# Output's start overlapped with the end of decode, and decode's joint sums moved into the output slabs

## The chip, the cores and the metric

One core of one Trainium2 chip runs the whole kernel. The metric is the device time of one execution in microseconds, lower is better. Engines are named as the profile names them: PE (TensorE), DVE (VectorE), ACT (ScalarE), POOL (GpSimd), SP (SyncE, here the queue that issues nearly all DMAs).

## What is computed

One decoder layer on 512 prompt rows and 8 x 4 sample rows, model width 2048, float32. An input projection feeds three mixers: differential attention (A, 4 heads), sparse attention (B, 4 heads, three branches) and an mLSTM (C, 8 heads). The last stages of the kernel, which the change touches, are the decode attention of the samples and the output product:

```
oa = rms_norm(oa, a_out_g) * (1.0 - lam_init)
ya = oa * silu(az)                      # group A
yb = (sum over 3 branches of gate * o_branch) * silu(bz)   # group B, gate = sigmoid(bg)
yc = rms_norm(h, c_out_g) * gates       # group C
y  = x + concat(ya, yb, yc) @ w_out     # (544, 2048) @ (2048, 2048)
```

The decode attention runs each sample batch over 4096 cached keys in pages, and its partial softmaxes are joined with running maxima and sums at the end.

## The kernel before, in words

The program is a chain of stages; each stage (`Stage`) frees its semaphores and ends with a barrier of all engines (line 94). The order of the work inside a stage is written out by hand for each engine, which is an in-order queue; semaphores tie them together.

**Decode** (`decode_attend`, line 1594). It goes through N = 80 steps: 8 batches with eight groups of four pages, one window and one step of new rows each. Each step loads its pages (2.5 MB, SP), turns keys (PE), scores, takes maxima (DVE), exponentials (ACT), turns them back and sums the values (PE, lines 1829 to 1845); ACT copies the sums out (`copy_o`). Per batch DVE combines the partial results in seven parts (`finish`, lines 2044 to 2077): weights, two scalings of `ob` (line 2071, nine and eleven columns of 128) and three sums (line 2076). After the last batch come the joint sums over the branches: transposes of maxima and sums (lines 1876, 1877), a joint exponential (1972), the scaling of `os_` (2121), six gathers of 512 columns on PE (1879, 1887) with copies on ACT and DVE, and twelve stores of 16 KB to `o_att` by SP (1727), awaited.

**Output** (`output`, line 3074). w_out's 2048 columns are cut into four slabs of 512 (j = 0 to 3), its 2048 rows into eight chunks of 256 (c = 0 to 7); a group is g = 8 j + c. Weights are split into a high half in the short matmul format (`high_w` on ACT, line 3279) and a low half (`low_w` on DVE, 3366), the activations likewise (`mhi`, `mlo`), and each product is three matmuls (3442 to 3444), so that a group costs 4 tiles x 2 x 3 = 24 matmuls of 512 columns. The rows come in five tiles: 0 to 3 of the prompt, and tile 4 with the 32 sample rows (`TURN`, `LAST` = 4). A tile is loaded (`load_tile`: `hc` 512 KB, `att` 1 MB, `zab` 512 KB, `zc` 2 x 256 KB, two buffers), POOL applies the gates to `att` (3254), ACT squares twelve heads and takes one root (`norms`, 3264 to 3271), DVE mixes (`mix`, 3322 to 3346: reciprocal, four products, three operations on group B, eight products on C), PE turns four quarters of it (`turn`, 3432), ACT and DVE make the high and low halves (`high`, `low`, 3288 and 3359).

Slab 0 goes tile by tile, since tile t + 1 is being mixed while tile t is multiplied: it is turned after chunk 5 of tile t. Slabs 1 to 3 go chunk by chunk with all four tiles in each. The sample rows (tile 4) are turned in slab 1's first group and multiplied by the unsplit weights, 16 small matmuls (3454) a group; for slab 0, which they missed, the weights are loaded a second time into one buffer `wx` and multiplied every third group. `add_x` (3368) adds x to a finished tile's product and so frees its PSUM bank; the first product of the next slab waits for it (3474). SP stores y and reads the next x in the second group of each slab (3193 to 3196, 3187), each read waiting for its own store to have landed. SP issues a weight chunk four groups ahead, once its buffer has been used (3175).

## Time and profile before

| what | us |
|---|---|
| three runs, median (lowest to highest) | 1827.3 (1820.32 to 1835.65) |
| profiled execution, span of its instructions | 1829.8 |
| PE busy in it | 1633.6 |
| output stage, from its first load (1582.1) to the end | 247.7 |

The profiled execution's time outside its span is not recorded. In windows the columns are the stretch, its length, then busy us (x instructions) of PE, PE weight loads, DVE, ACT and POOL, the granted PE clock as a share of full speed, the share of the DMA engines' time in use and GB/s. In timelines the columns are start, duration, engine, line, operation, written <- read, shapes, count, and in brackets the idle time before it with what ended it. In the chain they are start, duration, engine, tile and line. In the page's fifth part they are the group, then busy us and mean ns of one, then idle us before it and what ended most of it. In the DMA table they are the issue, its count, its size and the median us from issue to landing.

### The profile page before, as it was taken

The page shows a single profiled execution, that of the slowest core. Times are in us where ns is not written, and L with a number is a line of the kernel's source. Part 1 is how long each engine was busy: PE and PEld are TensorE (multiplying, and loading weights), DVE is VectorE, ACT ScalarE, POOL GpSimd, SP SyncE. Part 2 cuts the span into 40 slices and gives each one's busy share as a digit, 9 for nine tenths or more (in the row PEclk, how much of TensorE's full clock was granted, in tenths as well). Part 3 has the DMA queues.
Part 4 walks back from the last instruction along what each step waited for, and adds up shares of the span by engine and source line. Part 5 has one row for each costly group of instructions (what it writes and reads, how often), then busy time and mean ns, then how long its engine had stood idle before and what let it go on. Part 6 is the DMA issues. An engine that isn't in the chain of part 4 may idle for free. (4 is left out here: it accounts for less than half of the span.)

```text
span 1829.8 us, 38972 instructions
## 1 busy us (share of the span) xinstructions
PE 1633.6 (89%) x14817; PEld 1261.7 (69%) x14817; DVE 794.7 (43%) x1568; ACT 603.9 (33%) x1383; POOL 121.0 (7%) x186
## 2 busy tenths in 40 slices
PE   6999999999998899998977789899988988289998
PEld 5888888877777767776656666667666776067776
DVE  4212121263247444433435444665566556473221
ACT  4311121232122222321224154555555554252110
POOL 3000000053000001000012000000000000120000
PEclk9999999999999999998987698999999999589999
DMA  6556565685332324255246488999998996382343
GB/s 200 177 176 198 180 193 152 219 283 183 138 109 94 117 87 148 79 129 172 65 132 250 168 293 333 336 351 391 346 327 330 386 325 233 143 290 87 129 140 118
DMA packets 219686, 375.37 MB, mean 205 GB/s; under 512 B 42197, under 2 KB 122630, under 8 KB 218190
## 3 DMA queue, kind: packets, MB, share of 16 engines
q1 hardware_dynamic: 215390, 359.78, 57.7%
q0 software_dynamic: 3824, 11.02, 1.8%
q8 instruction: 118, 1.93, 0.4%
q10 hardware_dynamic: 288, 2.10, 0.4%
q14 instruction: 66, 0.54, 0.1%
HBM read 336.37 MB, written 40.71 MB: 206 GB/s over the span
## 5 line engine op out<-in xcount | busy, mean ns | idle before, releaser
L377 PE MATMUL pj_ps<-pj_whi,pj_xhi 128*128 128x512 f32 (+1 forms) x1024 | 413.7, 404 | 6.9 <-PEq L94 6.0
L378 PE MATMUL pj_ps<-pj_wlo,pj_xhi 128*128 128x512 f32 (+1 forms) x1024 | 399.3, 390 | 0.0
L379 PE MATMUL pj_ps<-pj_whi,pj_xlo 128*128 128x512 f32 (+1 forms) x1024 | 398.0, 389 | 0.0
L295 DVE TENSOR_TENSOR pj_wlo<-pj_w,pj_whi 128x1024 fp32r<-128x1024 f32 (+1 forms) x128 | 155.6, 1215 | 453.8 <-ACT pj_whi L253 452.1
L253 ACT ACTIVATE pj_whi<-pj_w 128x1024 fp32r<-128x1024 f32 (+1 forms) x128 | 132.2, 1033 | 506.0 <-DMA pj_w<-in_w_in 505.2
L377 PEld LDWEIGHTS pj_ps<-pj_whi,pj_xhi 128*128 128x128 f32 x1024 | 195.6, 191 | 66.5 <-issue 28.9
L379 PEld LDWEIGHTS pj_ps<-pj_whi,pj_xlo 128*128 128x128 f32 x1024 | 195.9, 191 | 40.2
L378 PEld LDWEIGHTS pj_ps<-pj_wlo,pj_xhi 128*128 128x128 f32 x1024 | 195.9, 191 | 33.9
L1899 ACT ACTIVATE da_kT<-da_tp 128x512 f32<-128x512 f32 x200 | 119.5, 597 | 176.6 <-PE da_tp L1766 165.5
L1991 DVE COPY da_kT<-da_tp 128x512 f32<-128x512 f32 x128 | 88.4, 690 | 91.8 <-PE da_tp L1766 91.3
L3442 PE MATMUL ou_ps<-ou_whi,ou_mhi 128*128 128x512 f32 x256 | 104.8, 409 | 6.7 <-DVE ou_wlo L3366 6.7
L3443 PE MATMUL ou_ps<-ou_wlo,ou_mhi 128*128 128x512 f32 x256 | 101.8, 397 | 0.0
L3444 PE MATMUL ou_ps<-ou_whi,ou_mlo 128*128 128x512 f32 x256 | 100.9, 394 | 0.0
L1766 PE MATMUL da_tp<-all_ident,at_early_a 128*128 128x128 f32 x512 | 77.5, 292 | 13.9 <-DMA at_early_a<-in_cache_a_kv 11.8
L3366 DVE TENSOR_TENSOR ou_wlo<-ou_w,ou_whi 128x1024 fp32r<-128x1024 f32 x32 | 40.6, 1287 | 97.5 <-ACT ou_whi L3279 97.4
L1766 PEld LDWEIGHTS da_tp<-all_ident,at_early_a 128*128 128x128 f32 x512 | 60.5, 149 | 23.9 <-DMA at_early_a<-in_cache_a_kv 15.4
L1766 PE MATMUL da_tp<-all_ident,da_pa 128*128 128x128 f32 x512 | 72.9, 279 | 2.1 <-DVE da_kT L1991 1.8
L1780 PE MATMUL da_sa<-da_kT,at_qa 128*32 128x512 f32 x512 | 68.8, 609 | 4.2 <-ACT da_kT L1899 4.2
L3279 ACT ACTIVATE ou_whi<-ou_w 128x1024 fp32r<-128x1024 f32 x32 | 33.5, 1058 | 112.7 <-DMA ou_w<-in_w_out 108.9
L2006 DVE TENSOR_REDUCE da_nm<-da_sa 128x1 f32<-128x512 f32 x64 | 44.1, 689 | 60.8 <-PE da_sa L1780 60.6
L343 PE MATMUL pj_ps<-pj_w,pj_xs 128*32 128x128 f32 (+1 forms) x2048 | 67.7, 273 | 0.0
L1766 PEld LDWEIGHTS da_tp<-all_ident,da_pa 128*128 128x128 f32 x512 | 56.2, 141 | 12.9 <-issue 6.3
(552 smaller groups left out, 2217.1 us busy)
## 6 DMA issues: line engine op xcount, KB each, us to landing
at_early_a<-in_cache_a_kv SPq DMA_DIRECT2D x128, 512.0 KB, 6.6
da_pa<-in_cache_a_kv SPq DMA_DIRECT2D x128, 512.0 KB, 6.4
pj_w<-in_w_in SPq DMA_DIRECT2D x120, 512.0 KB, 4.6
px_pages<-in_cache_b_kv SPq DMA_DIRECT2D x256, 128.0 KB, 2.5
at_early_b<-in_cache_b_kv SPq DMA_DIRECT2D x128, 128.0 KB, 6.4
da_pb<-in_cache_b_kv SPq DMA_DIRECT2D x128, 128.0 KB, 6.5
ou_w<-in_w_out SPq DMA_DIRECT2D x32, 512.0 KB, 4.2
proj<-pj_out SPq DMA_DIRECT2D x52, 256.0 KB, 4.9
```

The source lines that it names most:

```text
L253: act.activation(self.whi[:, g % self.RING, :, 0:n], self.w[:, g % self.RING, :, 0:n], ACT.Copy).then_inc(self.whi_ready, 1)
L295: dve.tensor_tensor(self.wlo[:, r, :, 0:n], self.w[:, r, :, 0:n], self.whi[:, r, :, 0:n], ALU.subtract).then_inc(self.wlo_ready, 1)
L377: pe.matmul(acc, hi, high, start=kc == 0, stop=False)
L378: pe.matmul(acc, hi, low, start=False, stop=False)
L379: last = pe.matmul(acc, lo, high, start=False, stop=kc == KC - 1)
L1766: last = pe.transpose(bank[:, c, :], src, k.ident[:])
L1780: last = pe.matmul(out, k.qa[:, b, h, :], keys, start=True, stop=True)
L1899: act.activation(kT[:, j, :].rearrange("p (c n) -> p c n", c=4), tp[tp_at["key", n, x] % 2][:], ACT.Copy).then_inc(act_copied, 1)
L1991: dve.tensor_copy(kT[:, j, :].rearrange("p (c n) -> p c n", c=4), tp[tp_at["key", n, x] % 2][:]).then_inc(dve_copied, 1)
L3442: pe.matmul(ps[t][:], hi, wh, start=kc == 0, stop=False)
L3443: pe.matmul(ps[t][:], hi, wl, start=False, stop=False)
L3444: last = pe.matmul(ps[t][:], lo, wh, start=False, stop=kc == KC - 1)
```

## The change

It moves the buffers that output's first loads need into a stage `fr` that lives from before decode to the end, and spreads output's start and decode's end over each other:

- Gates (their loads on POOL, their sigmoid on ACT) are done before and at the start of decode. `load_tile(0)`, `load_tile(1)` and weight chunks 0 to 2 are issued by SP in decode's last steps, each into buffers that decode has done with. ACT squares tile 0 and takes its root, and squares group C of tile 1, between and behind its last work of decode; POOL weighs tile 0 there.
- The last batch's scaling of eleven columns goes from DVE to ACT (`weigh_last`, eleven instructions).
- Decode's joint sums, gathers, copies and twelve stores move into slab 1 of output: transposes after its first group (g = 8), the share's transpose after g = 10, gathers after g = 8 and g = 12. SP stores at g = 13 (`store_attended`) and, once they have landed, loads tile 4, x of the samples and `wx` 0 and 1 at g = 14. ACT squares tile 4 after `high_w(15)`, DVE mixes it after `low_w(16)`.
- Tile 4 is turned after g = 16 (`LATE` = 16). The samples' products are 16 raw ones in slabs 2 and 3 and 16 with `wx` (two buffers), one of each in every group of slabs 2 and 3.
- In output's start the four quarters of tile 0 alternate with the low halves of weight chunks 0 to 3 on DVE and with the high halves on ACT; chunks 4 to 7 come before tile 1's mixing.

The core of the diff (each engine's order; removed lines of output are those of the kernel shown above):

```diff
-                place = d.o_att[SEQ:ROWS, :].rearrange("(b t) n -> t b n", t=DT)
-                sp.wait_ge(out_act, 3)
-                sp.wait_ge(out_dve, 3)
-                for x in range(3):
-                    for h in range(HA):
-                        c = 512 * x + HEAD * h
-                        sp.dma_start(place[:, :, c:c + HEAD], oo[4 * h:4 * h + 4, x, :, :]).then_inc(stored, 16)
-                sp.wait_ge(stored, 16 * 3 * HA)
+                sp.wait_ge(summed, at[DB - 1, "win", 0] + 1)
+                out.load_w(sp, 2)
+                sp.wait_ge(guest.stored, 16 * PT)
+                for u in range(2):
+                    sp.wait_ge(summed, at[DB - 1, "page", NG - RING + u] + 1)
+                    out.load_tile(sp, u)
+                sp.wait_ge(scored_b, N)
+                for g in range(2):
+                    out.load_w(sp, g)
 
             @block.gpsimd
             def _(pool):
                 for _ in guest.pool(pool):
                     pass
...
+                def weigh_last():
+
+                    i = (DB - 1) % 2
+                    act.wait_ge(weighed, DB)
+                    act.wait_ge(o_copied, N)
+                    for c in range(S0, NC):
+                        last = act.activation(ob[:, i, c, :], ob[:, i, c, :], ACT.Copy, scale=wt[:, i, c:c + 1])
+                    last.then_inc(last_weighed, 1)
+
+                out.act_gates(act)
                 act.wait_ge(consts_ready, 1)
                 tiles = guest.act(act)
                 for n in range(N + 9):
                     if 3 <= n < N + 3:
                         copy_o(n - 3)
+                    if n == N + 1:
+                        out.square_c(act, 0, 3, 6, sa)
                     copy_turn(n, 0)
                     if 1 <= n <= N:
...
+                    if n == N:
+                        act.wait_ge(exped_a, len(a_steps))
+                        out.square_c(act, 0, 0, 3, sa)
+                    if n == N + 1:
+                        out.square_c(act, 0, 6, HC, sa)
+                        out.square_a(act, 0, 0, 1, sa)
                     if n >= G + 3 and (n - 3) % G == 0 and (n - 3) // G <= DB:
...
+                        if b == DB - 1:
+                            weigh_last()
...
+                out.square_a(act, 0, 1, HA, sa)
+                out.root(act, 0)
+                out.square_c(act, 1, 0, HC, sa)
...
+                        if part == 3 and b == DB - 1:
+                            dve.wait_ge(last_weighed, 1)
+                            return
...
+                    for g in range(3, NP):
+                        load_w(g)
+                    load_tile(2)
+                    for t in range(PT):
+                        load_x(0, t)
+                    load_tile(3)
+                    for g in range(NP, NP + RING):
+                        load_w(g)
+                    for t in range(PT - 1):
+                        store(0, t)
+                    for t in range(PT - 1):
+                        load_x(1, t)
+                    for j in range(1, NSL):
+                        for c in range(NP):
+                            g = NP * j + c
+                            if g + RING < SLOTS:
+                                load_w(g + RING)
+                            if c == 1:
+                                for t in (3,) if j == 1 else range(PT):
+                                    store(j - 1, t)
+                                for t in (3,) if j == 1 else range(PT):
+                                    load_x(j, t)
+                                if j == NSL - 1:
+                                    store_samples(2, 1)
+                                    store_samples(0, 2)
+                            if g == NP + 5:
+                                store_attended()
+                            if g == NP + 6:
+                                sp.wait_ge(att_stored, 16 * 3 * HA)
+                                load_tile(LAST)
+                                for i in range(4):
+                                    sp.dma_start(out4[NS * i:NS * i + NS, :, :],
+                                                 d.x_sample.rearrange("r (j i n) -> i r j n", i=4, n=Q)[i]).then_inc(x_loaded[PT], 16)
+                                load_again(0)
+                                load_again(1)
+                            if g > LATE and g - LATE + 1 < LATE:
+                                load_again(g - LATE + 1)
+                    store_samples(3, 3)
+                    for t in range(PT):
+                        store(NSL - 1, t)
+                    store_samples(1, 4)
+                    for t in range(5):
+                        sp.wait_ge(stored[t], (16 if t < PT else 64) * NSL)
+
+                @block.gpsimd
+                def _(pool):
...
+                    act.wait_ge(self.gain_ready, 1)
                     for q in range(4):
+                        high_w(q)
+                        high(0, q)
+                    for g in range(RING, NP):
+                        high_w(g)
+                    self.square_a(act, 1, 0, HA, ps[PT])
+                    self.root(act, 1)
+                    for u in range(1, PT):
+                        if u + 1 < PT:
+                            self.square_c(act, u + 1, 0, HC, ps[PT])
+                            self.square_a(act, u + 1, 0, HA, ps[PT])
+                            self.root(act, u + 1)
+                        for q in range(4):
+                            high(u, q)
+                    for g in range(NP, SLOTS):
+                        high_w(g)
+                        if g == NP + 3:
+                            act.wait_ge(j_centred, 1)
+                            act.activation(joint[:, 1, :], joint[:, 0, :], ACT.Exp).then_inc(j_exped, 1)
+                            copy_out(0)
+                            copy_out(1)
+                        if g == NP + 6:
+                            copy_out(2)
+                        if g == NP + 7:
+                            self.square_c(act, LAST, 0, HC, ps[PT])
+                            self.square_a(act, LAST, 0, HA, ps[PT])
+                            self.root(act, LAST)
+                        if g == LATE + 1:
+                            high(LAST, 0)
...
+                    parts = (lambda: mix_a(0), lambda: mix_b(0), lambda: mix_c(0, 0), lambda: mix_c(0, 1))
                     for q in range(4):
+                        parts[q]()
+                        low_w(q)
+                        low(0, q)
+                    for g in range(RING, NP):
+                        low_w(g)
+                    for u in range(1, PT):
+                        mix(u)
+                        for q in range(4):
+                            low(u, q)
+                        if u > 1:
+                            add_x(0, u - 2)
+                    add_x(0, 2)
+                    for g in range(NP, NP + AHEAD):
+                        low_w(g)
+                    add_x(0, 3)
+                    for g in range(NP, SLOTS):
+                        if g + AHEAD < SLOTS:
+                            low_w(g + AHEAD)
+                        if g == NP + 1:
+                            join_maxima()
+                            join_sums()
+                        if g == NP + 2:
+                            scale_parts()
+                        if g == NP + 4:
+                            for x in range(3, 6):
+                                copy_out(x)
+                        if g == NP + 6:
+                            mix(LAST)
+                        if g % NP == NP - 1:
+                            j = g // NP
+                            for t in range(PT):
+                                add_x(j, t)
+                            if g > LATE:
+                                dve.wait_ge(raw_used, NP * (j - 1))
+                                add_samples(j, ps[PT])
+                                dve.wait_ge(wx_used, NP * (j - 1))
+                                add_samples(j - 2, tp[0])
...
+                    for j in range(1, NSL):
+                        for c in range(NP):
+                            g = NP * j + c
+                            pe.wait_ge(wlo_ready, g + 1)
+                            for t in range(PT):
+                                if c == 0:
+                                    pe.wait_ge(y_ready[t], j)
+                                multiply(j, c, t)
+                            if g == NP:
+                                pe.wait_ge(low_ready, 4 * PT)
+                                pe.transpose(tp[0][0:2 * DB, 0:P], self.mm[:], k.ident[:])
+                                pe.transpose(tp[0][0:2 * DB, P:2 * P], self.ll[:], k.ident[:]).then_inc(j_turned, 1)
+                                gather(0)
+                                gather(1)
+                            if g == NP + 2:
+                                pe.wait_ge(j_shared, 1)
+                                pe.transpose(tp[0][:, 2 * P:2 * P + 2 * DB], joint[:, 3, :],
+                                             k.ident[0:2 * DB, 0:2 * DB]).then_inc(j_back, 1)
+                            if g == NP + 4:
+                                pe.wait_ge(j_ready, 2)
+                                pe.wait_ge(out_act, 2)
+                                for x in range(2, 6):
+                                    gather(x)
+                            if g < LATE:
+                                continue
+                            if g == LATE:
+                                turn(LAST)
                                 pe.wait_ge(ms_ready, 3)
+                            if g == LATE + NP:
+                                pe.wait_ge(y_ready[PT], 1)
+                            multiply_samples(ps[PT], w[g % RING], c).then_inc(raw_used, 1)
+                            x = g - LATE
+                            pe.wait_ge(wx_loaded[x % 2], 16 * (x // 2 + 1))
+                            if x == NP:
+                                pe.wait_ge(y_ready[PT], 2)
+                            multiply_samples(tp[0], wx[x % 2], c).then_inc(wx_used, 1)
```

## Rows read from the trace of the kernel before

**Rows 1.** Windows of 20 us: decode's last, the gap, one in output's slab 2
```profile
1540.00:1560.00 20.00, 10.38 (x183) 7.40 (x175) 12.65 (x29) 5.71 (x18) 0.00 (x0) 0.89 0.01 2
...
1560.00:1580.00 20.00, 9.64 (x15) 1.62 (x15) 7.83 (x14) 2.07 (x4) 0.00 (x0) 0.67 0.05 10
...
1720.00:1740.00 20.00, 20.00 (x141) 15.48 (x140) 3.67 (x3) 3.18 (x3) 0.00 (x0) 1.00 0.52 171
```

**Rows 2.** Timeline: decode's end, joint sums, stores, and output's first load
```profile
1554.00 3.02 DVE L2071 TENSOR_TENSOR da_ob<-da_ob,da_wt 128x1152 f32<-128x1152 f32 x2
...
1559.05 2.40 DVE L2076 TENSOR_REDUCE da_os<-da_ob 128x128 f32<-128x1152 f32 x2
...
1572.79 1.02 PE L1887 MATMUL da_po<-da_os,at_four 128*16 128x512 f32 x2
...
1574.61 4.16 SPq L1727 DMA_DIRECT2D o_att<-da_pa  x12
...
1582.06 0.35 SPq L3160 DMA_DIRECT2D ou_hc<-h_c  x1
```

**Rows 3.** Timeline: output's start, from the gates to the first product
```profile
1589.18 0.24 ACT L3298 ACTIVATE ou_bg<-ou_bg 128x48 f32<-128x48 f32 x1 [5.54 <-DMA ou_bg<-proj]
...
1593.04 1.28 ACT L3271 ACT_TABLE_LOAD   x1
...
1594.74 0.23 DVE L3327 RECIPROCAL ou_rn<-ou_root 128x12 f32<-128x12 f32 x1 [3.05 <-ACT ou_root L3271]
...
1603.62 6.68 DVE L3366 TENSOR_TENSOR ou_wlo<-ou_w,ou_whi 128x1024 fp32r<-128x1024 f32 x4
...
1605.25 0.80 PE L3442 MATMUL ou_ps<-ou_whi,ou_mhi 128*128 128x512 f32 x1 [3.05 <-DVE ou_wlo L3366]
```

**Rows 4.** PE's timeline in slab 0, first tile
```profile
1616.96 0.80 PE L3442 MATMUL ou_ps<-ou_whi,ou_mhi 128*128 128x512 f32 x1 [3.68 <-DVE ou_wlo L3366]
...
1620.12 0.51 PE L3443 MATMUL ou_ps<-ou_wlo,ou_mhi 128*128 128x512 f32 x1
...
1626.63 0.39 PE L3444 MATMUL ou_ps<-ou_whi,ou_mlo 128*128 128x512 f32 x1
```

**Rows 5.** DVE's timeline, mixing of tile 4: its first and its last group
```profile
1659.36 0.21 DVE L3327 RECIPROCAL ou_rn<-ou_root 32x12 f32<-32x12 f32 x1
...
1662.69 2.17 DVE L3342 SCALAR_TENSOR_TENSOR ou_hc<-ou_hc,ou_rn,ou_zc 32x128 f32<-32x128 f32 x8
```

**Rows 6.** Page, part 5: high and low halves of output's weights
```profile
L3366 DVE TENSOR_TENSOR ou_wlo<-ou_w,ou_whi 128x1024 fp32r<-128x1024 f32 x32 | 40.6, 1287 | 97.5 <-ACT ou_whi L3279 97.4
L3279 ACT ACTIVATE ou_whi<-ou_w 128x1024 fp32r<-128x1024 f32 x32 | 33.5, 1058 | 112.7 <-DMA ou_w<-in_w_out 108.9
```

**Rows 7.** Chain that ended last, slab 1: samples' products of groups 10 to 12
```profile
1685.74 0.57 PE ou_ps L3454 x16
...
1692.02 0.57 PE ou_ps L3454 x16
...
1698.70 0.57 PE ou_ps L3454 x16
```

**Rows 8.** Tile view of output's `hc`: landing
```profile
DMA to landing us min/median/max: 4.0/6.2/13.3
```

**Rows 9.** SP's timeline in output's slabs: stores of y and reads of x
```profile
1680.52 0.47 SPq L3193 DMA_DIRECT2D out<-ou_out  x1
...
1684.77 0.34 SPq L3187 DMA_DIRECT2D ou_out<-in_x_prompt  x1
...
1782.96 2.55 SPq L3193 DMA_DIRECT2D out<-ou_out  x4
...
1788.10 2.91 SPq L3187 DMA_DIRECT2D ou_out<-in_x_prompt  x4
```

**Rows 10.** DMA table of output: weights
```profile
ou_w<-in_w_out SPq DMA_DIRECT2D x32, 512.0 KB, 4.2
ou_wx<-in_w_out SPq DMA_DIRECT2D x8, 512.0 KB, 5.0
```

807 lines of the change are left out of this document (380 added, 427 removed).

## The prediction

> **What bounds the kernel now.** I read the granted clock and busy shares in windows first, then the timelines of decode's end and of output's start, then the chain of waits in output, last SP's own timeline and the DMA table. The windows show two states. In slabs 1 to 3 of output PE is busy all the time at full clock (20.00 of 20.00) with the DMA queues half idle: there PE's work is the bound, and every microsecond in which PE waits is lost. Before it lies a hole: from 1540 to 1560 the DMA share is 0.01, and from 1560 to 1580 PE has 15 instructions at a clock of 0.67 [rows 1]. The hole is a chain: DVE combines decode's last batch until 1561.5, the joint sums and twelve stores run until 1578.8, output's first load is issued at 1582.06 [rows 2], gates, squares and root let DVE begin on tile 0 at 1594.74, and the first product starts at 1605.25 [rows 3]. That chain is what the change attacks. What it has to be weighed against is what it puts into slabs 1 to 3, where nothing is free.
>
> **Decode's end.** Loads of tiles 0 and 1 and of weight chunks 0 to 2 (6.5 MB) go into the idle queue of the 1540 window [rows 1]. At the page loads' pace (350 to 390 GB/s in the page's slices of decode) and with the second tile's load issued behind the last steps but two they are in by about 1559, an estimate. ACT takes eleven of the twenty scalings of the last batch off DVE: its two products last 3.02 us together [rows 2], 1.6 of it goes, and ACT's queue of squares gives some 0.6 back by delaying its copies. DVE ends near 1560.5, ACT (twelve squares, table, root, eight squares) at the same time. From the last store's issue to output's start 3.3 us passed, about half of it the store's landing and half the stage exits [rows 2]; only the exits remain, so output starts at 1562 where it was 1582. The joint sums' 13 us and the stores are gone from here, the gate load (waited for 5.54 us) and tile 0's squares too [rows 3].
>
> **Output's first tile.** What is late next is DVE. From its reciprocal at 1594.74 to the start of the low halves of the weights at 1603.62 lie 8.9 us of mixing and low halves of tile 0 [rows 3]. The change puts the low halves of the chunks between the quarters; three stand ahead of the last quarter, 1.67 us each beside POOL (6.68 for four) [rows 3]. First product: 1562 + 8.9 + 5.0 = 1576, against 1605.25: 29 us won. In the kernel before, the first tile's row of products lasts from 1605.25 to 1626.9 and holds a wait of 3.68 us for chunk 4 and a second stretch at half clock behind it (until 1620.12, some 1.6 us lost) [rows 3, 4]. In the new order chunks 4 to 7 come before tile 1's mixing, so that wait and its slow stretch go; but tile 1's mixing then ends only at 1562 + 15.6 (first tile) + 4 x 1.29 (page's row of L3366) + 5.5 (one mixing [rows 5, 6]) + 0.8, near 1589, and PE must turn tile 1 before chunks 6 and 7. Row 0 ends near 1593.4. Won so far: 33.5 us. Tiles 1 to 3 of slab 0 keep their order; I take them at no change.
>
> **PE's added and removed work.** Six gathers of 512 columns move into slab 1, 1.02 us by the last one in decode [rows 2], and three small transposes, 0.8 together. The samples' products: before 24 groups of 16 products at 0.57 and 8 more at 0.40 (periods 6.28 and 6.68 [rows 7]), after 16 groups with both: 16.9 against 15.5. Together +5.5 us. All of it is on the path, since PE has no gap there [rows 1].
>
> **Wait A, slab 2's start.** Tile 4 (the samples) can be loaded only when the gathers have been copied and stored. A group of slab 1 takes 6.28 - 0.57 = 5.7 us [rows 7]. Counted from the slab's start: fifth group and all gathers done at 5 x 5.7 + 6.9 = 35.4, copied 36.1, twelve stores issued 40.3 (4.16 [rows 2]), landed 42, `hc` in at 46 (4.0, the least that such a load took [rows 8]), twelve squares 3.5 (from the gates at 1589.5 to the table load), table and root 1.7 [rows 3]: 51.2. On ACT `high_w(16)` is queued behind these squares, on DVE `low_w(16)` behind that and `mix(LAST)` behind it; `add_x(1, 0)`, which frees PSUM for slab 2, is behind all. So 1.06 + 1.29 [rows 6], 5.5 for the mixing (1659.36 to 1664.86 [rows 5]), `low_w(17)` 1.29 and the sum 0.7: 61.0. PE is there at 8 x 5.7 + 6.9 = 52.5. It waits 8.5 us. After the wait of 3.68 us PE ran at half clock for 3.2 us [rows 4]; that costs another 1.6. A: +10.1, between 5 and 15 as the load takes 0 to 9 us.
>
> **Wait B, group 18, and wait C, group 26.** The samples' second weights `wx` now come each group, with two buffers. Chunk x is issued by SP one group ahead, but in the second group of a slab its issue stands behind four stores and four reads of x, each read waiting for its store to land. From store to read 4.25 us passed (1680.52 to 1684.77), four stores take 2.55, and where the reads were held by landings they took 2.91 [rows 9]. SP gets to `load_again(2)` 7.5 us after group 17, it lands 5.0 us later [rows 10]: 12.5. PE wants it 0.4 + 6.28 after group 17: it waits 5.8 us, with the clock 7.4. In group 26 eight sample stores (twice 2.55) stand ahead as well: 17.6 against 6.7, 10.9 us, with the clock 12.5. In the kernel before this never showed, as `wx` was wanted every third group only. Bounds: if the queue lets the reads pass without waiting (5.0 us for stores and reads), B is 3 and C 8; if landing takes 8 us, 9 and 14.
>
> The Trainium skill ("DMA: Bandwidth & Descriptors", Anatomy of one DMA) gives a DMA about 2.0 us plus its bytes at 436 GB/s, 3.2 us for a chunk of 512 KB; the rows show 4.2 and 5.0 [rows 10]. By the page B and C would each be 1.8 us shorter and the sum 3.6 lower.
>
> **Small ones.** Gates at decode's start: a table load of 1.28 [rows 3] while ACT waits for constants, and one more before the first exponential, on the path: +0.7, between 0 and 2.6. Four small loads on POOL ahead of decode: POOL is idle, nothing. The end: same stores, the sums 0.4 earlier: -0.4. In slab 1 the exponential and the root change ACT's table twice; the first is hidden by ACT's idle time, the second counted in A.
>
> The skill ("ScalarE: Activation LUTs", What ACT_TABLE_LOAD costs) puts a switch at 1.28 us plus a drain of 1.38. Here the root followed its load without that drain [rows 3]. By the page A would be 1.4 longer, the sum 1.4 higher.
>
> **Sum.** -33.5 + 5.5 + 10.1 + 7.4 + 12.5 + 0.7 - 0.4 = +2.3 us, against a span of 1829.8: 1832.1. What lies around the span isn't shown; the span is 2.5 above the median of the three runs, 1827.3, so the same sum on the median gives 1829.6. I forecast 1829.6: the hole at output's start is halved and given back as three waits and added work in slabs 1 to 3. A change of under 1% (18 us) is about what a measurement of this kernel can tell from none.
>
> **Rivals.** (1) The waits don't come: SP or the queues run ahead enough for `wx`, or tile 4 is in early. For it: the queues are half idle there. Against: the waits follow from the order written down, not from bandwidth. Without B and C the sum is 2.3 - 19.9, 1809.7; without A as well 1799.6. Chance 0.22, in most of it over 1% faster. (2) `wx` late in every group, the slower side. From issue (0.5 us after a group's end) to use are 6.2 us; the row has 5.0 [rows 10]. It decides from a landing of 6.2 us: at 7.7, twelve groups lose 1.5 each, 18 us more, 1847.6. Against: two chunks a group are 1 MB in 6.7 us, half of what the queues moved in decode. Chance 0.10. (3) The head start fails: ACT, stalled on `hc` between two copies of decode's last steps, holds PE and DVE, or the loads land late because they queue. At worst it eats 10 us of the 33.5: 1839.6. The idle window [rows 1] speaks against it. Chance 0.06. The forecast has 0.62.
>
> **How the numbers follow.** The forecast's own range from the bounds of A, B and C is 1816 to 1840. Extended to rival 1's partial cases and rival 2's milder ones it is 1804 to 1845. Over 1% faster is below 1809: 0.21. Over 1% slower, above 1845.6: 0.10. Within: 0.69.
>
> **What would show it.** Right: first product of output near 1576, slab 0's first row done near 1593; a wait of PE of 8 to 9 us before the first product of slab 2, released by `add_x`; waits on `wx` of about 6 and 11 us in the third group of slabs 2 and 3; half clock behind each; gathers of about 1 us. Wrong: no PE gap over 2 us behind slab 0 (rival 1), a gap in each group (rival 2), output's start later than 1566 (rival 3).

## The result, and the profile after

The changed kernel takes 1843.3 us (median of 12 runs, 1835.2 to 1848.1), the one before 1829.0 (12 runs): ratio 1.0073 [1.0055, 1.0092], 14 us slower. That is a change of under 1%, as forecast, and within the range, but the sum had +2.3. Ratios are taken over undisturbed executions; of the ten of `e2_mix_after_add` one, at 3153 us, is not among them. The rest of this document asks where the missing 12 us are, and whether each wait has the cause that the prediction gave it.

The page of the changed kernel, its head and the granted clock in 40 slices of 46 us:

```profile
span 1844.3 us, 39009 instructions
...
PEclk8999999999999999999987699999999999798898
```

Slice 35 holds output's start (7; in the kernel before it holds the gap ahead of output, at 5, with an 8 in the next one). In three of the slices behind it, where the page of before has only nines, stands an 8. Windows show what stands there; columns are the window, its length, busy time of PE, PEld, DVE, ACT and POOL, granted clock, DMA share and GB/s.

```profile
1540.00:1560.00 20.00, 12.76 (x231) 9.19 (x231) 11.26 (x28) 13.41 (x56) 3.05 (x3) 0.97 0.89 337
1560.00:1580.00 20.00, 3.34 (x12) 2.14 (x12) 15.64 (x21) 9.57 (x26) 3.14 (x3) 0.50 0.27 83
...
1700.50:1704.00 3.50, 3.48 (x8) 2.80 (x9) 1.67 (x3) 0.00 (x0) 0.00 (x0) 0.50 0.00 0
...
1724.60:1734.70 10.10, 0.06 (x4) 0.00 (x0) 0.07 (x1) 0.00 (x0) 0.00 (x0) 0.74 0.77 233
1734.70:1739.00 4.30, 4.29 (x24) 3.21 (x25) 1.23 (x1) 1.06 (x1) 0.00 (x0) 0.50 0.12 47
```

The idle DMA window of [rows 1] is full now (0.89 against 0.01). In return PE, which was busy for all 20.00 us of a window in slab 2 [rows 1], does nothing for 10 us at 1724.6, and runs at half clock (0.50, 1.2 of 2.4 GHz) behind it and behind the wait before 1700.5.

Decode's end and output's start, DVE and SP (compare [rows 2, 3]):

```profile
1556.95 1.36 DVE L2061 TENSOR_TENSOR da_ob<-da_ob,da_wt 128x1152 f32<-128x1152 f32 x1
1559.30 4.42 DVE L2066 TENSOR_REDUCE fr_kept<-da_ob 128x128 f32<-128x1152 f32 x3 [0.99 <-ACT da_ob L1929]
1565.69 0.23 DVE L3400 RECIPROCAL ou_rn<-fr_root 128x12 f32<-128x12 f32 x1 [1.97 <-PEq L95]
1565.95 3.20 DVE L3405 SCALAR_TENSOR_TENSOR fr_front<-fr_front,ou_rn 128x128 f32<-128x128 f32 x4
```
```profile
1555.88 3.32 ACT L1929 ACTIVATE da_ob<-da_ob,da_wt 128x128 f32<-128x128 f32 x11
```
```profile
1565.56 0.37 SPq L3115 DMA_DIRECT2D ou_w<-in_w_out  x1
```

ACT's eleven scalings take 3.32 us, so DVE, done with its nine after 1.36, waits 0.99 for them and is done at 1563.72. Output's first load is at 1565.56, where it was at 1582.06. The first products of DVE in output last 3.20 us for four.

The three waits of PE in the slabs behind (idle time in brackets):

```profile
1734.71 1.08 PE L3572 MATMUL ou_tp<-fr_kept 128*32 128x128 f32 x16 [10.05 <-DMA fr_kept<-in_w_out]
```

and in part 5 of the page, for slab 2's first product:

```profile
L3560 PE MATMUL ou_ps<-ou_whi,ou_mhi 128*128 128x512 f32 x256 | 106.7, 417 | 8.7 <-DVE ou_out L3458 8.7
```

The third, in slab 3's third group (1790.57 to 1799.25), is 8.68 us long and also for `wx`.

From the starts of PE's products in both profiles comes this account (us). Decode began 2.8 later in the changed kernel's profile; the profiles of the kernels below, which are alike up to there, differ by more (1038.8 to 1052.1). So experiments are read mostly by the length of output's stage, from its first load (before: of `hc`, after: of a weight chunk) to the end of the span.

| stretch | before | after | difference | forecast |
|---|---|---|---|---|
| up to decode's start | 1040.6 | 1043.3 | +2.8 | 0 |
| decode's start to output's | 541.5 | 522.2 | -19.3 | -19.4 |
| output's start to end of tile 0's row | 44.8 | 38.0 | -6.8 | -13.4 |
| rest of slab 0 | 38.2 | 38.2 | 0.0 | 0 |
| slabs 1 to 3, with the waits | 155.0 | 192.5 | +37.6 | +35.5 |
| end | 9.8 | 10.0 | +0.2 | -0.4 |
| sum | 1829.8 | 1844.3 | +14.5 | +2.3 |

### The profile page after: what moved, and what is told of

Its sections match the earlier page's. It is cut to its first block and busy times, and to the rows that moved or that the text cites. A ratio compares the mean times of both kernels' runs of the same rounds, so it can differ in the third digit from the quotient of the medians.

```text
span 1844.3 us, 39009 instructions
## 1 busy us (share of the span) xinstructions
PE 1635.2 (89%) x14817; PEld 1267.5 (69%) x14817; DVE 794.3 (43%) x1567; ACT 610.6 (33%) x1397; POOL 120.9 (7%) x186
## 5 line engine op out<-in xcount | busy, mean ns | idle before, releaser
L1871 ACT ACTIVATE fr_kT<-da_tp 128x512 f32<-128x512 f32 x200 | 119.4, 597 | 167.8 <-PE da_tp L1753 164.5
L1978 DVE COPY fr_kT<-da_tp 128x512 f32<-128x512 f32 x128 | 88.3, 690 | 93.0 <-PE da_tp L1753 92.7
L1753 PE MATMUL da_tp<-all_ident,fr_front 128*128 128x128 f32 x640 | 93.5, 285 | 23.8 <-DMA fr_front<-in_cache_a_kv 16.1
L1753 PEld LDWEIGHTS da_tp<-all_ident,fr_front 128*128 128x128 f32 x640 | 72.4, 145 | 38.2 <-DMA fr_front<-in_cache_a_kv 20.0
L1767 PE MATMUL da_sa<-fr_kT,at_qa 128*32 128x512 f32 x512 | 69.0, 610 | 4.2 <-ACT fr_kT L1871 4.2
L3560 PEld LDWEIGHTS ou_ps<-ou_whi,ou_mhi 128*128 128x128 f32 x256 | 50.9, 199 | 24.4 <-DVE ou_wlo L3450 9.3
L344 PEld LDWEIGHTS pj_ps<-pj_w,pj_xs 128*32 128x32 f32 x2048 | 50.9, 109 | 20.0 <-issue 19.8
```

What stands on the lines that cost most here:

```text
L344: last = pe.matmul(self.ps[4][NS * q:NS * q + NS, 0:n], self.xs[:, kc, :], self.w[:, x % self.RING, i, n * q:n * q + n], start=kc == 0, st ...
L1753: last = pe.transpose(bank[:, c, :], src, k.ident[:])
L1871: act.activation(kT[:, j, :].rearrange("p (c n) -> p c n", c=4), tp[tp_at["key", n, x] % 2][:], ACT.Copy).then_inc(act_copied, 1)
L1978: dve.tensor_copy(kT[:, j, :].rearrange("p (c n) -> p c n", c=4), tp[tp_at["key", n, x] % 2][:]).then_inc(dve_copied, 1)
L3560: pe.matmul(ps[t][:], hi, wh, start=kc == 0, stop=False)
```

## The experiments

All start from the changed kernel and compute the whole result. "Row end" is the end of the first tile's row of products (the start of the next tile's first product), "A" the wait before slab 2, "B" and "C" those for `wx` in slabs 2 and 3; all are from one profile each and counted from output's start where a time is meant.

| kernel | first product | row end | A | B | C | output's stage | ratio to before |
|---|---|---|---|---|---|---|---|
| before | 23.2 | 44.8 | 0 | 0 | 0 | 247.7 | 1 |
| after | 16.5 | 38.0 | 8.66 | 10.05 | 8.68 | 278.7 | 1.0073 |
| e1_wx_first | 16.5 | 36.9 | 8.67 | 5.54 | 7.64 | 273.0 | 1.0036 [1.0013, 1.0059] |
| e2_mix_after_add | 16.5 | 38.0 | 0 | 8.65 | 8.46 | 265.0 | 1.0008 [0.9989, 1.0027] |
| e3_joint_early | 16.5 | 37.3 | 0 | 9.20 | 8.73 | 267.3 | 1.0034 [1.0005, 1.0062] |
| e4_pool_later | 15.6 | 32.4 | 8.79 | 10.44 | 8.50 | 274.8 | 1.0068 [1.0043, 1.0092] |
| e5_quarters_first | 12.3 | 39.1 | 8.58 | 9.69 | 8.71 | 279.8 | 1.0090 [1.0048, 1.0131] |
| e6_weigh_dve | 16.5 | 37.2 | 8.13 | 9.41 | 8.60 | 277.4 | a single run, 1837.5 us |
| e12_reads_later | 16.5 | 37.7 | 10.42 | 3.30 | 2.55 | 267.6 | 1.0016 [1.0003, 1.0029] |
| e9_spread | 16.5 | 37.6 | 8.04 | 0 | 0 | 254.3 | 0.9974 [0.9944, 1.0003] |
| e10_best | 15.6 | 32.5 | 0 | 0 | 0 | 239.6 | 0.9889 [0.9831, 0.9946] |
| e11_best_quarters | 12.6 | 37.5 | 0 | 0 | 0 | 243.5 | 0.9881 [0.9853, 0.9908] |

**B and C: who holds `wx`.** SP's timeline of the changed kernel in slab 2:

```profile
1718.46 2.51 SPq L3266 DMA_DIRECT2D out<-ou_out  x4
1723.00 4.01 SPq L3261 DMA_DIRECT2D ou_out<-in_x_prompt  x4
1727.05 0.43 SPq L3250 DMA_DIRECT2D fr_kept<-in_w_out  x1
```

Four stores, then SP sits until the first has landed (4.5 us from its issue), then four reads, and only then `wx`, 9.0 us behind the group's weight chunk. It lands at 1734.7, 7.65 us later.

`e1_wx_first` puts `wx` ahead of stores and reads:

```diff
                                 load_w(g + RING)
+                            if g > LATE and g - LATE + 1 < LATE:
+                                load_again(g - LATE + 1)
                             if c == 1:
...
-                            if g > LATE and g - LATE + 1 < LATE:
-                                load_again(g - LATE + 1)
```

> Only SP's order in output changes: the load of the samples' second weights for the next group is issued right behind the weight chunk, ahead of the stores of y and the reads of x. Theory (the waits of 10.0 us in group 18 and 8.7 us in group 26 are made by SP's queue order, each with a stretch at half clock behind it): both waits vanish, slabs 2 and 3 lose some 21 us, the kernel ends near 1822 us, ratio to the kernel before 0.996. Rival (the loads are late because the queues are busy in these groups, landing took 7.7 us once): waits of 3 us or more stay in the same places and the gain is under 12 us, ratio 1.001 or more.

```profile
1718.35 0.47 SPq L3250 DMA_DIRECT2D fr_kept<-in_w_out  x1
1718.87 2.57 SPq L3266 DMA_DIRECT2D out<-ou_out  x4
1724.98 3.71 SPq L3261 DMA_DIRECT2D ou_out<-in_x_prompt  x4
1728.74 0.43 SPq L3115 DMA_DIRECT2D fr_pw<-in_w_out  x1
1729.21 0.47 SPq L3250 DMA_DIRECT2D fr_kept<-in_w_out  x1
```

Neither expectation came out as written: the wait did not go, and it did not stay in its place, it moved one group on (5.54 us at 1731.2, 7.64 at 1792.4). SP is in stores, landings and reads for 9.8 us (8.6 in the changed kernel), and now the next group's chunk stands behind them (1729.21). With two buffers only one chunk can be ahead. The stage got 5.7 shorter, not 21; that is the rival's size (under 12 us), so this run alone doesn't tell SP's order from a slow landing.

`e12_reads_later` keeps all bytes and takes the holding away: reads and sample stores are issued one group after the stores, whose landing is then over.

```diff
-                                for t in (3,) if j == 1 else range(PT):
-                                    load_x(j, t)
+                                if j == 1:
+                                    load_x(1, 3)
+                            if c == 2 and j > 1:
+                                for t in range(PT):
+                                    load_x(j, t)
...
```

> The changed kernel, but in slabs 2 and 3 the four reads of x (and the eight sample stores) are issued one group later than the four stores of y; the bytes and their number stay, only SP's holding for landings goes, since by then the stores have landed. In the changed kernel's profile SP issues wx of chunk 2 9.0 us behind the weight chunk of its group (stores 2.5, reads 4.0 and the holding between), and it lands 7.65 later; PE wants it 6.7 behind: wait 10.05. Theory (SP's order and holding): chunk 2 is issued 3.3 behind the weight chunk; with the same landing the wait is 4.3 us, with a landing of 5 it is 1.7, and the chunk of the next group, behind the reads, may wait 1 to 4 us more. Same in slab 3, there with the sample stores: 4 to 6 us. Stage 264 to 270 us against 278.7, time 1829 to 1835. Rival (the landing, made long by stores and reads in the queues, is the cause, however SP issues): the sum of the waits in each slab stays at 8 us or more, stage 275 or more.

```profile
1723.52 1.08 SPq L3250 DMA_DIRECT2D fr_kept<-in_w_out  x1
```

B fell to 3.30 and C to 2.55, with no further wait in the next groups; the stage is 267.6, as SP's holding would have it and not the landing. The two parts can be told apart here: `wx` is issued 2.8 us behind its group's chunk instead of 9.0, but still takes 7.1 to land (7.65 before); in slab 3 it is issued 3.0 behind instead of 11.0 and lands even later, 6.1 against 4.3. So what B and C lost came from the issue, and SP's order with its waits for landings is the larger part of both; the 3.30 that is left of B is landing. (A is 10.42 in this run: `hc` of tile 4 landed 5.7 us behind its issue and not 3.9, and A grew by the same 1.8.)

`e9_spread` spreads the same transfers: one store (groups 2 to 5 of a slab) and one read (groups 3 to 6) per group, always behind `wx`.

```diff
...
+                            if j > 1:
+                                if 2 <= c < 2 + PT:
+                                    load_x(j, c - 2)
+                                if 1 <= c < 1 + PT:
+                                    store(j - 1, c - 1)
+                                if j == NSL - 1 and c == 6:
+                                    store_samples(2, 1)
+                                if j == NSL - 1 and c == 7:
+                                    store_samples(0, 2)
```

> The changed kernel with SP's order in slabs 2 and 3 of output spread: in each group first the weight chunk, then wx, and behind them one store of y (groups 2 to 5 of the slab) and one read of x (groups 3 to 6, one group after its store), the eight sample stores in groups 7 and 8. In the changed kernel's profile output takes 278.7 us from its first load to the end; PE waits 10.05 us in the third group of slab 2 and 8.68 in that of slab 3, and the clock is halved behind each. Theory (SP is held by reads that wait for their stores, with wx behind them): both waits go, with their slow stretches some 22 us: output's stage 256 to 258 us, time near 1821, ratio to the kernel before 0.995. Rival (the queues: a chunk takes longer to land than the group's 6.7 us while stores and reads share them): each of the groups with a store waits 1 to 3 us, the stage stays above 268, time 1833 or more.

```profile
1715.01 0.37 SPq L3115 DMA_DIRECT2D fr_pw<-in_w_out  x1
1715.43 0.47 SPq L3250 DMA_DIRECT2D fr_kept<-in_w_out  x1
1715.94 0.47 SPq L3261 DMA_DIRECT2D ou_out<-in_x_prompt  x1
1716.45 0.43 SPq L3266 DMA_DIRECT2D out<-ou_out  x1
```

Both waits are gone. The stage is 24.4 us shorter (278.7 to 254.3, two more than expected); of the kernel's time the interval just reaches 1. The waits themselves were 18.7; the two groups from the wait on, which took 25.87 and 24.63, take 13.34 now, so each slow stretch had cost 2.5 (25.87 - 10.05 - 13.34) and 2.6. This also tells against rival 2: with a chunk of `wx` in every group no group waits.

**A: the mixing of tile 4 ahead of the sums.** The chain in the changed kernel, from SP's stores to the sum that frees slab 2's banks:

```profile
1676.11 4.17 SPq L3281 DMA_DIRECT2D o_att<-fr_kept  x12
...
1681.88 0.32 SPq L3106 DMA_DIRECT2D fr_front<-h_c  x1
...
1685.78 0.27 ACT L3162 ACTIVATE ou_ps<-fr_front 32x128 f32<-32x128 f32 x1 [11.47 <-DMA fr_front<-h_c]
...
1689.42 1.28 ACT L3177 ACT_TABLE_LOAD   x1
1690.71 0.30 ACT L3177 ACTIVATE fr_root<-fr_ss,all_eps 32x12 f32<-32x12 f32 x1
1690.92 1.99 ACT L3339 ACTIVATE ou_whi<-fr_kT 128x1024 fp32r<-128x1024 f32 x2
1692.00 1.23 DVE L3450 TENSOR_TENSOR ou_wlo<-fr_kT,ou_whi 128x1024 fp32r<-128x1024 f32 x1 [14.84 <-ACT ou_whi L3339]
1693.14 0.21 DVE L3400 RECIPROCAL ou_rn<-fr_root 32x12 f32<-32x12 f32 x1
...
1696.47 2.17 DVE L3424 SCALAR_TENSOR_TENSOR fr_front<-fr_front,ou_rn 32x128 f32<-32x128 f32 x8
1698.57 1.21 DVE L3450 TENSOR_TENSOR ou_wlo<-fr_kT,ou_whi 128x1024 fp32r<-128x1024 f32 x1
1699.70 2.46 DVE L3458 TENSOR_TENSOR ou_out<-ou_out,ou_ps 128x512 f32<-128x512 f32 x4
```

DVE stands 14.84 us for ACT, ACT 11.47 for `hc`; the sum comes at 1699.70, and PE, done at 1691.86, starts slab 2 at 1700.52.

`e2_mix_after_add` puts ACT's squares behind `high_w(17)` and `mix(LAST)` behind `add_x` of slab 1:

```diff
-                        if g == NP + 7:
+                        if g == LATE + 1:
                             self.square_c(act, LAST, 0, HC, ps[PT])
...
-                        if g == LATE + 1:
...
-                        if g == NP + 6:
-                            mix(LAST)
...
                                 add_x(j, t)
+                            if j == 1:
+                                mix(LAST)
```

> Tile 4's squares go behind the high half of group 17's weights on ACT, its mixing behind the four sums of slab 1 on DVE; its data arrive as before. Theory (the wait of 8.7 us at slab 2's start is the mixing standing in DVE's queue ahead of the sums): no wait before slab 2's first product; PE waits 2 to 4 us after group 16 to turn tile 4; 5 to 8 us less than the changed kernel, ratio to the kernel before 1.003 to 1.005. Rival (tile 4's data come late and whatever needs them waits as long): the wait of 8 to 9 us moves behind group 16 and the time stays, ratio 1.007.

```profile
1684.88 0.69 DVE L3457 TENSOR_TENSOR ou_out<-ou_out,ou_ps 128x512 f32<-128x512 f32 x1 [0.67 <-PE ou_ps L3561]
1685.48 0.21 DVE L3399 RECIPROCAL ou_rn<-fr_root 32x12 f32<-32x12 f32 x1
```

DVE now waits for PE and not PE for DVE; the mixing follows behind the sum, and the turn of tile 4 after group 16 finds it done. The wait of 2 to 4 us expected there did not come, so the gain is larger than the 5 to 8 us expected. A is 0, the stage 13.7 us shorter: 8.66 of wait, 2.3 of slow clock (first two groups 17.84 us in the changed kernel, 15.50 here), 1.6 less at B and C, and a microsecond spread over the rest.

`e3_joint_early` gets at the same wait from the other end, by an earlier start of the chain (gathers after g = 8 and 10, stores at 11, tile 4's loads at 12, squares at 14, mixing after `low_w(15)`). The transposes move too:

```diff
-                            if g == NP + 4:
+                            if g == NP + 2:
                                 pe.wait_ge(j_ready, 2)
...
-                            if g == NP + 5:
+                            if g == NP + 3:
                                 store_attended()
```

> The share's transpose goes from group 10 to 9, the gathers from group 12 to 10, copies, stores, loads of tile 4, squares and mixing follow one or two groups earlier. Nothing is left out. Theory (chain from the gathers to the first sum of slab 1 is too long by 8.7 us): tile 4 is mixed before slab 1 ends, no wait before slab 2's first product and no half clock behind it, 9 to 11 us less than the changed kernel, ratio 1.002. Rival (mixing in DVE's queue delays the sums wherever it is put, or the joint sums themselves stall PE when asked for earlier): a wait of 3 us or more at groups 9 to 11 or in front of group 13 to 16, gain under 5 us.

A is 0 here as well, the stage 267.3. That A hangs on the chain and not on something else at slab 2's start is shown from both ends.

**The row of tile 0.** `e4_pool_later` keeps POOL out of DVE's first products and of its mixing of tile 1; its weights for tile 1 wait until two quarters of tile 0 are mixed, those for tile 2 until all of tile 1 is:

```diff
                     for u in range(1, len(TURN)):
+                        if u == 1:
+                            pool.wait_ge(mixed, 2)
+                        if u == 2:
+                            pool.wait_ge(mixed, 8)
                         self.weigh(pool, u)
```

> POOL weighs tile 1 only after two quarters of tile 0 are mixed, tile 2 only after tile 1 is mixed. Theory (POOL's products slow DVE's while both run: the first four products of output took 3.20 us instead of 1.14, and tile 1's mixing lost 2.2 us): the first four take 1.1 to 1.3, the first product of output comes about 2 us earlier, slab 0's first row ends 2 to 4 us earlier, ratio to the kernel before about 1.005. Rival (the slow first products have another cause, such as engines starting after the stage's barrier): they stay at 3 us.

DVE's mixing of tile 1 and POOL's weights of tile 2 in the changed kernel; then, here, DVE's first products, its third quarter of tile 0 and its mixing of tile 1, and POOL's weights of tile 1:

```profile
1591.35 1.42 DVE L3414 TENSOR_TENSOR fr_front<-fr_front 128x512 f32<-128x512 f32 x1
...
1594.14 2.96 DVE L3424 SCALAR_TENSOR_TENSOR fr_front<-fr_front,ou_rn 128x128 f32<-128x128 f32 x8
```
```profile
1590.83 4.29 POOL L3147 TENSOR_TENSOR fr_front<-fr_front,fr_bg 128x512 f32<-128x512 f32 x3 [22.09 <-DMA fr_front<-o_att]
```
```profile
1554.85 1.14 DVE L3409 SCALAR_TENSOR_TENSOR fr_front<-fr_front,ou_rn 128x128 f32<-128x128 f32 x4
...
1563.16 2.32 DVE L3428 SCALAR_TENSOR_TENSOR fr_front<-fr_front,ou_rn 128x128 f32<-128x128 f32 x4
...
1579.34 0.69 DVE L3418 TENSOR_TENSOR fr_front<-fr_front 128x512 f32<-128x512 f32 x1
...
1580.67 2.18 DVE L3428 SCALAR_TENSOR_TENSOR fr_front<-fr_front,ou_rn 128x128 f32<-128x128 f32 x8
```
```profile
1560.80 4.02 POOL L3147 TENSOR_TENSOR fr_front<-fr_front,fr_bg 128x512 f32<-128x512 f32 x3 [20.32 <-DVE fr_front L3419]
```

The first four products take 1.14 us again, and the rival (they stay at 3 us) is out. But PE's first product comes only 0.9 earlier and not the 2 expected, since POOL's weights of tile 1, released behind the second quarter, now fall on the third: its four products take 2.32 (1.13 in the changed kernel). Tile 1's mixing is 2.2 us shorter (1.42, 1.41 and 2.96 became 0.69, 0.69 and 2.18), and the row ends 32.4 us behind output's start instead of 38.0: 0.9 before the first product, 4.7 in the row. 2.2 of the 4.7 is the mixing, the rest mostly the clock, as PE's rows show it. PE waited for the turn of tile 1 1.47, 1.17 and 0.82 us in the changed kernel and then ran at half clock to 1603; here, with 0.35 and 1.15, it stayed at full clock:

```profile
1598.60:1603.30 4.70, 4.70 (x13) 3.73 (x13) 3.86 (x10) 1.21 (x5) 0.00 (x0) 0.52 0.72 235
```
```profile
1584.00:1587.00 3.00, 3.00 (x16) 2.48 (x15) 2.68 (x8) 0.69 (x1) 2.00 (x2) 1.00 0.56 142
```

(the first line is the changed kernel, the second e4). The stage is 3.9 us shorter in the profile; the time of the whole kernel can't tell that from nothing (ratio 1.0068, the changed kernel's is 1.0073).

`e5_quarters_first` takes tile 0's quarters back to back on DVE, with the low halves of all chunks behind them, and on ACT likewise with the high halves (not shown):

```diff
                     for q in range(4):
                         parts[q]()
-                        low_w(q)
+                    for q in range(4):
                         low(0, q)
-                    for g in range(RING, NP):
+                    for g in range(NP):
                         low_w(g)
...
```

> The changed kernel with tile 0's four quarters mixed back to back and the low halves of the weights all behind them (the order of the kernel before), loads and everything else as changed. Theory (DVE's and ACT's turns: DVE waits four times 0.7 to 0.8 us for ACT between a low half of a chunk and that of a quarter, and three low halves of 1.22 stand ahead of the last quarter): the first product comes 3 to 4 us earlier than 16.4 behind output's start, the row of tile 0 ends 2 to 3 us earlier than 38.0 behind the start, stage 276. Rival (the new order is what keeps PE fed): first product 3 to 4 earlier, but a wait for a chunk or for the turn of tile 1 of 3 us or more appears in the row, its end is where it was or later, stage 278.7 or above.

```profile
1593.27 1.06 ACT L3339 ACTIVATE ou_whi<-fr_kT 128x1024 fp32r<-128x1024 f32 x1 [3.22 <-DMA fr_kT<-in_w_out]
```

The rival's outcome: first product 4.1 us earlier, but waits of 2.61 and 2.85 for tile 1's turn, and the row's end 1.1 later. A part of it is the loading: chunk 4 goes into the buffer that the first low half frees, so SP issues it 12.3 us behind output's start and not 4.8, ACT waits 3.22 us for it, and DVE stands 1.82 and 1.63 us for ACT at chunks 4 and 5. The row ends with DVE's path to tile 1's turn, and the alternating order, which frees the buffers early, is not what the kernel loses by.

`e6_weigh_dve` undoes `weigh_last` (DVE scales all twenty columns):

```diff
-                        if b == DB - 1:
-                            weigh_last()
...
-                        if part == 3 and b == DB - 1:
-                            dve.wait_ge(last_weighed, 1)
-                            return
```

> The changed kernel with the last batch's scalings all on DVE again (ACT's eleven removed). In the changed kernel DVE's nine take 1.36, ACT's eleven 3.32, and DVE waits 0.99 for them; in the kernel before DVE did all twenty in 3.02. Theory (DVE's combination sets output's start): DVE is done 0.7 us later, and output's first load in output's stage comes 0.7 later behind the last product of decode. Rival (ACT's tail sets it: the eleven, squares, table, root and eight squares run until 0.15 us after DVE's end): ACT ends 3.3 earlier, and output starts no later or earlier.

```profile
1549.40 3.02 DVE L2056 TENSOR_TENSOR da_ob<-da_ob,da_wt 128x1152 f32<-128x1152 f32 x2
```

From the last batch's exponential (1548.09 here) to output's start (1558.41) it is 10.3 us; in the changed kernel, from 1555.63, it is 9.9. So the eleven scalings on ACT seem to be worth 0.4 us: the theory's direction, about half its size, on one profile each, which doesn't settle it.

**Together.** `e10_best` is e9, e2 and e4 in one kernel.

> e9's spread order together with two edits: tile 4 is mixed only behind the sums of slab 1 (squares, root and mixing moved past add_x, as in e2_mix_after_add), and POOL's weights for tiles 1 and 2 wait until DVE has mixed the tile before (as in e4_pool_later). If the three causes are separate, their gains add: from 278.7 us of the changed kernel's output stage 13.7 go with the wait ahead of slab 2, some 22 with the two waits for wx, 3 to 5 with POOL out of DVE's way: stage 239 to 242 us, against 247.7 in the kernel before, on top of 16 to 20 us won ahead of output; time 1804 to 1808, ratio 0.988. Rival: the groups of slab 2 then want the samples' turn and two chunks at once, and a new wait of 5 us or more stands in group 17 or 18: stage 245 or more, ratio 0.991 or above.

1804.0 us, ratio 0.9889 [0.9831, 0.9946] from four runs: 1.1% faster than before, 1.8% than the changed kernel (0.9889 against 1.0073). The stage is 239.6 us. The single gains are 24.4 + 13.7 + 3.9 = 42.0; 1.6 of that is counted twice (e2's share in B and C), and one wait of 1.18 for `wx` is left in slab 3, which makes 39.2 (measured: 39.1). The three causes are separate. Slabs 2 and 3 are at full clock:

```profile
1684.40:1739.90 55.50, 54.51 (x465) 42.95 (x463) 18.64 (x30) 10.25 (x13) 0.00 (x0) 1.00 0.54 173
1739.93:1793.40 53.47, 52.28 (x420) 40.97 (x416) 9.61 (x10) 5.30 (x5) 0.00 (x0) 1.00 0.54 170
```

`e11_best_quarters` adds e5's order to it.

> e10_best with tile 0's quarters back to back as in e5_quarters_first. In e5 the first product came 4.1 us earlier and the row of tile 0 ended 1.1 later, with POOL beside DVE at both mixings. Theory (DVE's total work up to tile 1's turn sets the row's end, and PE in between starts earlier only to wait): the row ends within 1 us of e10's 32.5 behind output's start, stage 239 to 241 us, no better than e10. Rival (with POOL out of the way the early first product counts): row's end 2 to 3 us earlier, stage 237, time near 1801.

```profile
1563.69 4.55 DVE L3433 SCALAR_TENSOR_TENSOR fr_front<-fr_front,ou_rn 128x128 f32<-128x128 f32 x8
```
```profile
1576.85 1.06 ACT L3347 ACTIVATE ou_whi<-fr_kT 128x1024 fp32r<-128x1024 f32 x1 [3.16 <-DMA fr_kT<-in_w_out]
```

Neither expectation holds: the row ends 5.0 us later than in e10, though the first product is 2.9 earlier. As in e5, chunk 4 goes into the buffer that the first low half frees, here issued at 1572.80, so ACT waits 3.16 us for it and 2.20 for chunk 5, and behind tile 1's turn PE takes the end of the row at half clock. Nor is POOL out of the way: its weights of tile 1, released behind the second quarter, fall on DVE's eight products of tile 0, which take 4.55 us for 2.18. So the rival's condition was not met, and it stays untested. The kernel's time is e10's (1805.4 and 1804.0). The alternating order stays.

## Why the prediction was right or wrong

- **Output's start at 1562: right.** It came 19.3 us earlier against decode's start; 19.4 with the gates had been forecast. Inside it DVE's end gained 0.5 and not 1.0 (1563.72 - 1043.34 = 520.4 against 520.9), since DVE waits 0.99 for ACT. The first exponential is 1.4 later behind the copy ahead of it than before (1.91 us against 0.49; forecast 0.7, within its bounds).
- **Tile 0's row: the step that failed.** "Row 0 ends near 1593.4" should have been 1601 (1603.57 less the 2.8 of decode's later start). The first product came 16.5 behind the start and not 14, and the row took 21.6, not 17.4. I had POOL's cost in the low halves [rows 3], where it did not fall (1.21 to 1.22 each, not 1.67), but not in DVE's first products (3.20 for 1.14) and tile 1's mixing (+2.2), and left out DVE's four waits of 0.7 to 0.8 for ACT in the alternating order and the stretch at half clock behind tile 1's turn. I had written of the slow stretch of [rows 4] that it goes; it went from chunk 4 and came back at the turn. Of the 12 us that the sum lacks 6.6 are here. e4 gets 5.6 of them back by moving POOL's work, though 1.2 us of POOL's cost comes back in its third quarter.
- **Added PE work +5.5: too high.** e9, which has neither B nor C, gives it: slab 1 50.1 before its wait against 53.4, slab 2 58.2 less A's slow stretch of 2.4 against 51.5, slab 3 52.1 against 50.1, together +3.0. The gathers followed one another at 0.86 us (1673.43 to 1674.29), not 1.02, but they are the smaller part: the groups that hold gathers and transposes are together 6.4 us over a bare group (5.44), against 6.9 forecast. The larger part is the samples' products, which I priced by the length of their rows (0.57 and 0.40). By the starts of the groups one set costs 0.8 us a group (6.24 against the bare 5.44), and two cost 1.28 in the kernel before (6.72) and 1.23 in e9 (6.67). Up to the last product the kernel before has 15 groups with one set and 8 with two, some 22 us, and e9 15 with two, some 18.5: about 4 us saved, where I had 1.4.
- **A, 8.5 us: right** (8.66), and by the chain described: e2 and e3 remove it from both ends. Every point of the chain and PE's arrival at slab 2 are 1.7 to 2.4 earlier than forecast, counted from the slab's start, so the difference stayed. The slow stretch cost 2.3, not 1.6.
- **B and C: right in cause and place, mis-sized.** B 10.05 instead of 5.8: `wx` was issued 9.0 and not 7.5 behind its group, and landed after 7.65 and not 5.0 [rows 10]. C 8.68 instead of 10.9: reads and sample stores took 2.27 and 3.67 us, not 2.91 and 5.1 [rows 9], and the landing was 4.3. Their sum, 18.7, is 2 us over the forecast's 16.7; the slow clock behind them 2.5 and 2.6 instead of 1.6 each. The Trainium skill ("DMA: Bandwidth & Descriptors", Anatomy of one DMA) gives its 2.0 us plus bytes at 436 GB/s for DMAs issued by GpSimd, and these chunks are issued by SP; taken for them all the same it would have had each in 3.2 us, an estimate. They landed after 7.65 and 4.3, and the sum would have been 3.6 further off.
- **The table loads: right.** ACT's root stands at 1690.71, right behind a load of 1.28 at 1689.42. The drain of 1.38 that the Trainium skill ("ScalarE: Activation LUTs", What ACT_TABLE_LOAD costs) adds does not appear here either: ACT's last square ends at 1689.40.
- **Rivals.** (1), waits that do not come, is refuted by the profile, (2), each group late, by e9, (3), a failed head start, by the first point. None of the three had the slowing at output's start that did come, that of DVE beside POOL.
- **The sum.** It fell into the range by its mechanism and not by luck: the gain, the added work and the three waits are all there. But errors partly cancelled: the row came 6.6 us dearer than forecast and A, B and C with their slow stretches 4.8, the added work 2.5 cheaper.
- 2.8 us of the profiles' difference lie ahead of decode's first load, where the change adds only the gates' loads on POOL. Whether some of the measured 14 is such drift is open: medians of 12 runs give 14.3, the profiles 14.5, and 11.7 from decode's start on.

## What to carry to other kernels

When loads of a deeper stage move into a queue that also stores results and reads into the buffers they leave, count the time for which the queue's engine is held for landings, and compare it with the buffers' lead: a load with one group of lead belongs into a group with little else, and stores and reads are spread one per group. A chain's last link should not stand ahead of the instruction that frees the next stage's banks when it can stand behind it. And work that is free on an idle engine (POOL) is not free when its neighbour (DVE) is what everyone waits for.

## What the runs showed that I had not expected

- POOL and DVE slow each other by an amount that depends on the operation. Beside POOL's weights DVE's four 128x128 products took 3.20 us (1.14 alone), its 128x512 additions 1.42 (0.69 alone), against 1.67 [rows 3] and 1.22 for the 128x1024 low halves. POOL's own three products took 3.14 beside the first of these and 4.29 beside the second (3.06 alone).
- Three waits of 1.47, 1.17 and 0.82 us within the turn of one tile were followed by half clock; two of 0.35 and 1.15 were not. The price of a slow stretch behind a wait of 8 to 10 us was 2.3 to 2.6 us of PE in the changed kernel, and a shorter wait was not cheaper: behind e12's waits of 3.30 and 2.55 the groups lost 2.7 and 2.3 us, behind e10's of 1.18 only 0.2.
- The same 512 KB chunk lands 4.3 us behind its issue in slab 3 and 7.65 behind eight transfers of 256 KB in slab 2, the chunks issued after that one 8.5 and 9.3:

```profile
fr_kept<-in_w_out SPq DMA_DIRECT2D x2, 512.0 KB, 8.4
fr_pw<-in_w_out SPq DMA_DIRECT2D x1, 512.0 KB, 8.5
```

These are rows of the DMA table of 1700 to 1740 us of the changed kernel (the 8.4 is the median of 7.6 and 9.3); for the chunk that lands in 4.3 see C above.
